# A PEER layer on one core: gate buffers lent to the gather of U rows, and all one-hot groups of tile 0 placed among the dots

## What is computed

```python
    q = _normalize((hf @ p['peer_wq']).reshape(t, PEER_HEADS, PEER_DKEY)).astype(h.dtype)
    s1 = jnp.einsum('thd,hkd->thk', q[..., :half], p['peer_subkeys'][:, 0])
    s2 = jnp.einsum('thd,hkd->thk', q[..., half:], p['peer_subkeys'][:, 1])
    v1, i1 = lax.top_k(s1, PEER_TOPK)
    v2, i2 = lax.top_k(s2, PEER_TOPK)
    cand_s = (v1[..., :, None] + v2[..., None, :]).reshape(t, PEER_HEADS, PEER_TOPK * PEER_TOPK)
    cand_i = (i1[..., :, None] * PEER_NKEYS + i2[..., None, :]).reshape(t, PEER_HEADS, PEER_TOPK * PEER_TOPK)
    best_s, pos = lax.top_k(cand_s, PEER_TOPK)
    idx = jnp.take_along_axis(cand_i, pos, axis=-1).reshape(t, PEER_HEADS * PEER_TOPK)
    gate = jax.nn.softmax(best_s.astype(F32), axis=-1).astype(h.dtype).reshape(t, PEER_HEADS * PEER_TOPK)
...
        act = jax.nn.gelu(jnp.einsum('td,tkd->tk', hb, p['peer_u'][ib]))
        return jnp.einsum('tk,tkd->td', act * gb, p['peer_v'][ib])
```

## Time and profile before

| | us |
|---|---|
| median of 3 runs | 3439.13 (3436.4 to 3443.51) |
| profiled execution | 3441.32 |
| its span in the profile | 3439.3 |
| TensorE busy | 3180.5 (92% of the span) |
| VectorE busy | 2065.9 (60%) |
| POOL busy | 996.8 (29%) |
| ScalarE busy | 659.6 (19%) |
| DMA, mean over the span | 271 GB/s |
| granted TensorE clock, mean | 0.97 of full speed |

### The profile page before, as it was taken

One profiled execution on the slowest core, in us unless ns is written; L12 is line 12 of the kernel. 1 busy time (PEld: TensorE's weight loads), 2 busy tenths in 40 slices (PEclk: granted clock), 3 DMA queues, 4 the chain that ended last, 5 costly groups with the idle time before them and its releaser, 6 DMA issues. The chain is left out here.

```text
span 3439.3 us, 36161 instructions
## 1 busy us (share of the span) xinstructions
PE 3180.5 (92%) x12755; PEld 2025.8 (59%) x12790; DVE 2065.9 (60%) x3590; ACT 659.6 (19%) x1176; POOL 996.8 (29%) x618
## 2 busy tenths in 40 slices
PE   6999999999999999999999999888667778999995
PEld 2467666675758576777644444566666667444442
DVE  6544444444434343566665534678889997665667
ACT  2312122121212121211100001223224445000000
POOL 0011112020202011200000001455666661775775
PEclk8999999999999999999999999999889999999999
...
GB/s 359 276 238 165 198 187 183 198 163 215 157 218 140 226 133 237 187 190 189 173 200 171 173 324 236 376 400 370 388 402 406 409 404 188 381 420 421 419 420 308
DMA packets 176746, 932.82 MB, mean 271 GB/s; under 512 B 24105, under 2 KB 38122, under 8 KB 94698
## 3 DMA queue, kind: packets, MB, share of 16 engines
...
HBM read 908.81 MB, written 22.28 MB: 271 GB/s over the span
## 5 line engine op out<-in xcount | busy, mean ns | idle before, releaser
L1079 PE MATMUL ps<-mT,ring 128*128 128x256 f32 (+1 forms) x4096 | 1168.9, 446 | 1.1 <-PEq L216 1.1
L1079 PEld LDWEIGHTS ps<-mT,ring 128*128 128x128 f32 x4096 | 774.9, 190 | 388.1 <-issue 318.3
L2222 POOL DMA_INDIRECT u_rows<-in_peer_u_dram,expert_indices x172 | 271.4, 1578 | 260.0 <-PE ps L2788 87.5
L2541 DVE CUSTOM_DVE_ANT_0 u_rows<-u_rows,yhy 128x2048 f32<-128x2048 f32 x130 | 294.1, 2287 | 57.0 <-DMA u_rows<-in_peer_u_dram,expert_indices 44.5
L2796 PE MATMUL ps<-mT,turned_rows 128*128 128x128 f32 x2016 | 293.5, 299 | 14.3 <-ACT turned_rows L2300 14.2
L711 POOL TENSOR_TENSOR dd<-mask_f,dt_g 128x1024 f32<-128x1024 f32 x16 | 30.4, 1897 | 933.0 <-DVE dt_g L981 932.4
L2796 PEld LDWEIGHTS ps<-mT,turned_rows 128*128 128x128 f32 x2016 | 272.4, 211 | 29.2 <-issue 26.5
L871 DVE SCALAR_TENSOR_TENSOR conv<-ps,tap_g,conv 128x510 f32<-128x510 f32 (+1 forms) x48 | 33.8, 704 | 338.7 <-ACT conv L732 338.7
L2300 ACT COPY turned_rows<-ps 128x512 f32<-128x512 f32 x252 | 143.7, 587 | 416.0 <-PE ps L2788 415.8
L2235 POOL DMA_INDIRECT scores<-in_v_rest_dram,expert_indices x128 | 178.4, 1394 | 131.8 <-PE ps L2839 49.5
L2611 DVE SCALAR_TENSOR_TENSOR turned_rows<-scores,expert_gate,turned_rows 128x1024 f32<-128x1024 f32 x118 | 151.7, 1288 | 91.2 <-DMA scores<-in_v_rest_dram,expert_indices 90.9
(11 more groups left out here) (409 smaller groups left out, 4427.0 us busy)
## 6 DMA issues: line engine op xcount, KB each, us to landing
...
yhy<-in_v_dense_dram SPq DMA_DIRECT2D x128, 512.0 KB, 6.5
...
ring<-in_w_mod_dram SPq DMA_DIRECT2D x32, 1024.0 KB, 10.8
...
```

What stands on the lines that cost most here:

```text
L1079: mm = nc.tensor.matmul(ps[:, k % 4, 0:n], m.ring[:, slot, kt * P:(kt + 1) * P], m.mT[:, kt, 0:n], start=(kt == 0), stop=(kt == KT - 1))
L2222: nc.gpsimd.indirect_dma_start(u_slot[j % NU], None, d.peer_u, bass.IndirectOffsetOnAxis(ap=eidx[:, j:j + 1], axis=0)).then_inc(u_in[j % N ...
L2541: nc.vector.tensor_tensor_reduce(out=u_slot[j % NU], in0=u_slot[j % NU], in1=h2[:, t, :], scale=1.0, scalar=0.0, op0=ALU.mult, op1=ALU.add ...
```

## The change

Rows 16 to 135 go round ten slots in place of six: the four gate rows are lent as slots 6 to 9, in the order `LENT_ORDER`. Row 16, the first in a gate row, waits for the query weights there to be used; all others wait for the row that had their slot before (`row_before`), and from row 136 on that is again row j - 6. ScalarE waits before its first copy into the gate rows until rows 132 and 135 have been taken. Second, four steps (39, 43, 47, 51) take two one-hot groups each, so that all 32 of tile 0 stand in steps 36 to 63; behind the dots only tile 1's remain, and TensorE turns tile 1's coefficients before their first group.

```diff
@@ -1914,7 +1914,7 @@
         HALF_D = D // 2
         h2 = m.yhy[:].rearrange("p a b -> p (a b)").rearrange("p (t n) -> p t n", n=D)
         gate_rows = m.gates[:].rearrange("p a b -> p (a b)").rearrange("p (s n) -> p s n", n=D)
-        u_slot = [m.u_rows[:, n, :] for n in range(SLOTS)] + [m.h[:, t, :] for t in range(TT)]
+        u_slot = [m.u_rows[:, n, :] for n in range(SLOTS)] + [m.h[:, t, :] for t in range(TT)] + [gate_rows[:, n, :] for n in range(4)]
         NU = len(u_slot)
         gt1, lng, lnb = u_slot[0], u_slot[1], u_slot[2]
         sh2, sc2 = gate_rows[:, 0, :], gate_rows[:, 1, :]
@@ -2062,6 +2062,25 @@
 
         N_DVE = dve_rows(ROWS - 1)
 
+        NSMALL, LENT_FROM, LENT_TO = SLOTS + TT, TOPK, TOPK + 12 * NU
+        LENT_ORDER = (6, 7, 8, 9, 4, 5, 0, 1, 2, 3)
+
+        def slot_of(j):
+
+            return LENT_ORDER[(j - LENT_FROM) % NU] if LENT_FROM <= j < LENT_TO else j % NSMALL
+
+        def row_before(j):
+
+            return max([i for i in range(j) if slot_of(i) == slot_of(j)], default=None)
+
+        def landed(j):
+
+            return 16 * sum(slot_of(i) == slot_of(j) for i in range(j + 1))
+
+        def await_row(engine, j):
+
+            engine.wait_ge(u_in[slot_of(j)], landed(j))
+
         def row_taken(engine, j):
 
             if on_pe(j):
@@ -2099,11 +2118,14 @@
         FIRST_SPREAD = NB * (PH + 1)
         GROUPS_4 = P // 4
 
+        DOUBLE = (39, 43, 47, 51)
+
         def spread_at(step):
 
-            return range(step - FIRST_SPREAD, step - FIRST_SPREAD + 1) if FIRST_SPREAD <= step < NB * UNITS else range(0)
-
-        LEFT_OVER = range(NB * UNITS - FIRST_SPREAD, GROUPS_4)
+            if not FIRST_SPREAD <= step < NB * UNITS:
+                return range(0)
+            first = step - FIRST_SPREAD + sum(d < step for d in DOUBLE)
+            return range(first, first + (2 if step in DOUBLE else 1))
 
         def hot_banks(k):
 
@@ -2213,14 +2235,17 @@
                 for j in range(ROWS):
                     if j % TOPK == 0:
                         pool.wait_ge(idx_v, j // TOPK + 1)
-                    if j >= NU:
-                        row_taken(pool, j - NU)
+                    if row_before(j) is not None:
+                        row_taken(pool, row_before(j))
+                    elif j >= LENT_FROM:
+                        pool.wait_ge(home_used, N_HOME)
+                        pool.wait_ge(h2_p, 2 * TT + 1)
                     elif j >= SLOTS:
                         pool.wait_ge(h_st[j - SLOTS], 16)
                         pool.wait_ge(h2_v, j - SLOTS + 1)
                     pool.sem_inc(pool_step, 1)
                     nc.gpsimd.indirect_dma_start(
-                        u_slot[j % NU], None, d.peer_u, bass.IndirectOffsetOnAxis(ap=eidx[:, j:j + 1], axis=0)).then_inc(u_in[j % NU], 16)
+                        u_slot[slot_of(j)], None, d.peer_u, bass.IndirectOffsetOnAxis(ap=eidx[:, j:j + 1], axis=0)).then_inc(u_in[slot_of(j)], 16)
                 for k in range(ROWS):
                     if k == 2:
                         pool.wait_ge(dot_v, N_DVE)
@@ -2348,6 +2373,8 @@
                             copy_by_pair(0)
                             act.wait_ge(m.w_used, START_Q + SQ_TILES - N_HOME)
                             act.wait_ge(home_used, N_HOME)
+                            row_taken(act, LENT_TO - 1)
+                            row_taken(act, LENT_TO - 4)
                         for n in spread_at(k):
                             second_one_hots(n)
                             if n:
@@ -2367,14 +2394,12 @@
                             copy_scores(done)
                         if new is not None:
                             copy_columns(new)
-                second_one_hots(LEFT_OVER[0])
-                copy_weights(LEFT_OVER[0] - 1)
                 gelu(UNITS - 1)
-                for k in range(LEFT_OVER[0] + 1, TT * GROUPS_4):
+                copy_weights(GROUPS_4 - 1)
+                copy_by_pair(1)
+                for k in range(GROUPS_4, TT * GROUPS_4):
                     second_one_hots(k)
-                    if k == GROUPS_4:
-                        copy_by_pair(1)
-                    if not by_dve(k - 1):
+                    if k > GROUPS_4 and not by_dve(k - 1):
                         copy_weights(k - 1)
                 copy_weights(TT * GROUPS_4 - 1)
 
@@ -2537,8 +2562,8 @@
 
                 def dot_row(j):
                     u, t = j // TOPK, j // (ROWS // TT)
-                    v.wait_ge(u_in[j % NU], 16 * (j // NU) + 16)
-                    nc.vector.tensor_tensor_reduce(out=u_slot[j % NU], in0=u_slot[j % NU], in1=h2[:, t, :], scale=1.0, scalar=0.0,
+                    await_row(v, j)
+                    nc.vector.tensor_tensor_reduce(out=u_slot[slot_of(j)], in0=u_slot[slot_of(j)], in1=h2[:, t, :], scale=1.0, scalar=0.0,
                                                    op0=ALU.mult, op1=ALU.add, accum_out=dots[:, u % 2, j % TOPK:j % TOPK + 1]).then_inc(dot_v, 1)
 
                 def take_diagonal(k):
@@ -2677,6 +2702,9 @@
                         for n in range(4):
                             if not on_pe(4 * k + n):
                                 dot_row(4 * k + n)
+                            if n == 0:
+                                for i in spread_at(k)[:-1]:
+                                    first_one_hots(i)
                         if k:
                             take_diagonal(k - 1)
                         if u < UNITS - 1:
@@ -2691,13 +2719,12 @@
                                 coefficients(u - 1)
                             if u in GROUPS_AT:
                                 normalise_queries(GROUPS_AT[u])
-                        for n in spread_at(k):
+                        for n in spread_at(k)[-1:]:
                             first_one_hots(n)
                         if (u, h) in ((PH - 1, 3), (UNITS - 2, 3)):
                             pair_polynomials(u // PH)
-                first_one_hots(LEFT_OVER[0])
                 coefficients(UNITS - 1)
-                for k in range(LEFT_OVER[0] + 1, TT * GROUPS_4):
+                for k in range(GROUPS_4, TT * GROUPS_4):
                     first_one_hots(k)
                     if by_dve(k - 1):
                         copy_late_weights(k - 1)
@@ -2782,7 +2809,7 @@
                 def turn_quarter(k, g):
                     if 4 * k + g >= 2:
                         pe.wait_ge(turn_a, 4 * k + g - 1)
-                    row = u_slot[(4 * k + 3) % NU]
+                    row = u_slot[slot_of(4 * k + 3)]
                     for a in range(4):
                         i = 4 * g + a
                         mm = nc.tensor.transpose(ps[:, g % 2, a * P:(a + 1) * P], row[:, i * P:(i + 1) * P], m.ident[:])
@@ -2799,7 +2826,7 @@
 
                 def row_by_pe(k):
                     j = 4 * k + 3
-                    pe.wait_ge(u_in[j % NU], 16 * (j // NU) + 16)
+                    await_row(pe, j)
                     turn_quarter(k, 0)
                     turn_quarter(k, 1)
                     if k >= 2:
@@ -2900,6 +2927,9 @@
                 for u in range(UNITS):
                     for h in range(NB):
                         k = NB * u + h
+                        for n in spread_at(k)[:-1]:
+                            key_distances(n + 1)
+                            spread_tokens(n)
                         if k < N_PE:
                             row_by_pe(k)
                         done, new = turns_at(u, h)
@@ -2913,15 +2943,14 @@
                             turn_by_pair(0)
                         if k == FIRST_SPREAD - 1:
                             key_distances(0)
-                        for n in spread_at(k):
+                        for n in spread_at(k)[-1:]:
                             key_distances(n + 1)
                             spread_tokens(n)
-                for k in range(LEFT_OVER[0], TT * GROUPS_4):
+                turn_by_pair(1)
+                for k in range(GROUPS_4, TT * GROUPS_4):
                     if k + 1 < TT * GROUPS_4:
                         key_distances(k + 1)
                     spread_tokens(k)
-                    if k == LEFT_OVER[0]:
-                        turn_by_pair(1)
                 pe.wait_ge(w_a, copied(TT * GROUPS_4 - 1))
                 pe.wait_ge(w_v, copied_by_dve(TT * GROUPS_4 - 1))
                 pe.wait_ge(diag_v, N_PE)
```

## The result

The changed kernel takes 3414.12 us (median of four runs, 3409.39 to 3417.53) against 3441.32 us for the kernel before beside it (3436.4 to 3444.51): ratio 0.9923, 95% interval 0.9911 to 0.9936. The forecast was 3417 us. A second series of the same kernel gave 3414.18 us and 0.9927 (0.9913 to 0.9941). The profiled execution took 3417.53 us, span 3415.6.

A forecast was written before the change was run, and what follows sets the result against it. VectorE and the DMA taking turns at waiting bound steps 9 to 33, VectorE's floor being higher. Terms -14.7 - 2.4 + 0 + 0.5 - 5.5 = -22.1 us, from 3439.1, gave 3417 us; range 3400 to 3431.

The forecast's parts named there:

- Gather and score waits: Steps 9 to 33: ten slots remove 14.7 us of VectorE's waits for gathered rows and 2.4 us for scores.
- Pair chain: Steps 32 to 35: pair rows are stored and reloaded in 52.5 us, so any gain is lost again; 0, within 4 us.
- Groups into the dots: Steps 39, 43, 47, 51: one added one-hot each, mostly hidden in waits for rows; 0.5 us lost, between 0 and 2.8.
- signs that I had named for a right prediction: Among them: steps 9 to 33 DMA at 400 GB/s or more, gather waits under 4 us, POOL's slot waits halved.
- Hand-over: From the first tile's last diagonal to tile 1's first one-hot: 10.9 us become about 5.4; gain 5.5, bounds 2.7 and 8.
- A, only the tail gains: Rival for steps 9 to 33: gather waits become score and TensorE waits one for one; 3434 us, chance 0.10.
- B, everything goes: Rival: score waits and pair chain also shrink as rows land earlier; 40.7 us gained, 3398 us, chance 0.08.
- the causes named in part 1: TensorE's query weights hold the score wait before unit 3; the pair rows' store and reload fixes the wait for them.
- C, POOL the bound: Rival for steps 9 to 33: gather issues grow dearer beside VectorE's dots, deciding from 2.57 us mean; 3452 us, chance 0.04.
- D, the DMA fuller than its bytes say: Rival for steps 9 to 33: a row costs 2.74 us, floor 273.7 us, only 8.5 us can go; 3426 us, chance 0.14.
- The rule of the Trainium skill that spoke against it: Steps 9 to 33: at 358 GB/s the DMA floor of 100 rows would be 293 us, the whole 3445 us.

The follow-up runs named there:

- both early lendings: The changed kernel with ten slots lent to rows 10 to 139 (3403.25 us) or to rows 9 to 138 (3403.06 us), not 16 to 135.

## Why the prediction was right

Time and sign were right, and so was the mechanism of the slots, which made the gain. The other half of the change was forecast at -5.0 us (+0.5 and -5.5) and gave nothing that can be told: the slots alone took 3414.87 and 3413.40 us, the whole change 3414.12 and 3414.18; with ten slots from row 10 the move made 3 us, within overlapping intervals. That the sum still came out within 3 us is in part luck.

- **Gather and score waits, -14.7 and -2.4 = -17.1.** The two profiles give -21.8. The table gives less: six slots took 282.2, 277.3 and 278.1 us (mean 279.2), ten slots from row 16 260.3, 261.1, 260.4, 260.2, 261.4 and 261.8 (mean 260.9), so -18.3. Of this term's miss 3 us are the long profile from which it was worked out. The loop was named rightly: slots full, POOL standing, DMA dry. The score wait before unit 3 stayed at 6.7; that before unit 5 went wholly, 4.8, where I took half.
- **Pair chain, 0 (-4 to +4).** Steps 34 to 36 took 32.7, 32.9 and 32.3 us with six slots, 29.7 to 30.7 with ten from row 16: 2 to 3 us gained. I took the lead to be lost there; a part was kept. The gain lies within the 4 us that I had allowed.
- **Groups into the dots, +0.5 (0 to 2.8).** This step failed. Steps 37 to 63 took 280.0, 278.3, 285.2, 280.2 and 279.1 us undoubled (mean 280.6), and 287.1, 286.5, 287.9, 281.8, 281.8 and 283.1 with the second group behind the first dot (mean 284.7): +4.1, and +7 in the changed kernel itself. The step said "the step after each of them begins a unit, where VectorE waits some 0.8 us for the first row" and "The move eats most of that wait", and priced VectorE's 0.69 us. The wait was read from one row: in the kernel before, the steps behind the four doubled ones begin with waits of 0, 0, 0.92 and 0.82 us, half the cover that I took. Above all it did not ask when the operand of the added one-hot is there. TensorE was said to have 87 us idle, "its part costs nothing"; but it is a step behind at that place, for the same late rows, so its idle time lies ahead of the work that VectorE needs. One of the signs that I had named for a right prediction, steps 34 to 63 within 3 us of 312.6, was missed for this (317.1 us).
- **Hand-over, -5.5 (2.7 to 8).** The path itself: 10.9 to 4.9 us, forecast 5.4. The window from there to the V stream fell by 6.0 in the pair of profiles, by 4.2 in the mean (57.1 over five, 52.9 over the seven with full rows). The path is not what falls short: it took 10.1 to 10.9 us in the five and 4.9 in the seven. What stands behind it, tile 1's groups, took 46.6 us in all five, but 48.2 to 48.3 in six of the seven; there the granted clock was 0.77 to 0.78 over the first 10 us, against 1.00 in the five. TensorE waits some 7 us at the end of the dots with the groups moved or not (7.05 us before, 6.91 in the second execution of the changed kernel) and then works at the lower clock level. Before, the lower level fell on the four groups of tile 0 (0.50 over the first 5.0 us of the hand-over); now much of it falls on tile 1's (in that second execution 0.51 over their first 4.5 us). I had moved "the 32 groups of tile 1" up "as they are", and some 1.6 us of the gain went there. In the changed kernel's first execution they did take 46.6 us.
- **The sum.** -18.3 - 2.4 + 4.1 - 4.2 = -20.8 us by means, -23.7 in the two spans, -27.2 by the medians of the first series and -24.5 by those of the second (3438.71 and 3414.18); forecast -22.1. Two gains taken too small, a cost taken too small and a gain taken too large nearly cancel. The time ahead of step 4, untouched, varies by 7 us between executions, so these sums can't be told apart.

The rivals. A, only the tail gains: excluded by the slots alone. B, everything goes: the waits for scores (6.7 of 11.5 us) and for pair columns (3.12 us on TensorE, 3.35 before) stayed, as the causes named in part 1 said; 3398 us was not reached. C, POOL the bound: its mean issue rose from 1.65 to 1.76 us, and the point from which it decides, 2.57, stayed far. D, the DMA fuller than its bytes say: in steps 9 to 33 it moved 419 GB/s at share 1.01, not 383 at 0.97, so the share hid gaps. In steps 37 to 63 the same doubt is half right: the stage hangs on rows, yet the share is 0.99 or 1.00 in executions that differ by 10 us and move 393 to 406 GB/s. The share doesn't tell them apart, the rate does.

The rule of the Trainium skill that spoke against it (DMA: Bandwidth & Descriptors, section Bandwidth, about 358 GB/s for each core of a pair) did not bind: 418 to 428 GB/s were read with this one core running. What two cores of a pair would get, no run here shows. POOL's issues cost the same with half the bytes on the DMA (1908 ns median in both), so it is not the bytes that make them dear; they are dear beside dots (2.05 us against 0.99). The Trainium skill (DMA: Bandwidth & Descriptors, section SWDGE vs HWDGE vs iDMA) names VectorE's lock on GpSimd's descriptor rings; the runs agree as far as the price goes with the dots, and whether it is that lock was not tried.

What stays open: why steps 37 to 63 take about 280 us in some executions and about 287 in others. Doubling makes the long one likelier (three of six with the one-hot behind the first dot at 286.5 or more; a seventh, with half the bytes only ahead of this stage, took 279.9), and the one-hots' waits go with it, but slots alone had 285.2 once without any, and eight slots and both early lendings, doubled, did not. Which slot order or phase decides was not settled.
